# Sample attention: the value blocks' loads are issued by ScalarE instead of SyncE

## The reference, cut to what matters

```python
K = jnp.concatenate([prev_k, k], axis=1)      # 1024 cached + 16 new rows, 8 heads of 64
V = jnp.concatenate([prev_v, v], axis=1)
F = jnp.cumsum(jnp.concatenate([prev_logf, logf], axis=1), axis=1)
s = jnp.einsum('bqhd,bkhd->bhqk', q, K) * scale
s = s + fblk[..., None] - fkT                 # forget terms
s = jnp.where(k_pos <= q_pos, s, -jnp.inf)
p = jax.nn.softmax(s, axis=-1)
o = jnp.einsum('bhqk,bkhd->bqhd', p, V)
b = o * silu(ag)                              # then concatenated, and x + mixed @ w_out
```

## Time and profile before

| | us |
|---|---|
| median of 3 runs | 1608.34 (1605.97 to 1609.19) |
| the profiled execution | 1604.41 |
| its span, first to last instruction | 1602.6 |
| PE busy | 1536.1 (96%) |
| DVE busy | 821.8 (51%) |
| ACT busy | 631.3 (39%) |
| POOL busy | 410.6 (26%) |
| mean granted clock of PE | 0.987 of 2.4 GHz |

### The profile page before, as it was taken

How to read it: one execution, slowest core, us unless ns; L and a number is a source line. 1 busy time by engine, 2 the same in 40 slices (tenths; PEclk the granted TensorE clock), 3 DMA queues, 4 the chain that set the end, 5 groups by cost and what they waited for, 6 DMA issues and landing times.

```text
span 1602.6 us, 24609 instructions
## 1 busy us (share of the span) xinstructions
PE 1536.1 (96%) x9264; PEld 1355.1 (85%) x9264; DVE 821.8 (51%) x2069; ACT 631.3 (39%) x1347; POOL 410.6 (26%) x706
## 2 busy tenths in 40 slices
PE   6999999999999899999999999999998999899999
PEld 5998888878799899898888888888887778688887
DVE  3333112232444422214988988888896788832221
ACT  4443121121211201113877877877975444410100
POOL 1110005555400000022444444444423355200000
PEclk9999999999999899999999999999999999899999
DMA  5433122121110200422133233233233665634441
GB/s 150 149 108 100 42 87 76 47 92 53 62 51 20 70 19 11 85 44 49 36 76 64 58 69 71 49 67 72 49 116 113 222 217 184 238 109 141 129 148 66
DMA packets 181511, 144.63 MB, mean 90 GB/s; under 512 B 104016, under 2 KB 140785, under 8 KB 181393
## 3 DMA queue, kind: packets, MB, share of 16 engines
q1 hardware_dynamic: 178880, 134.08, 28.8%
q10 hardware_dynamic: 2448, 8.91, 1.4%
q0 software_dynamic: 64, 0.07, 0.1%
HBM read 106.50 MB, written 36.53 MB: 89 GB/s over the span
## 4 chain that ended last, share of the span: by engine, by line
PE 52%; DVE 6%; ACT 4%; DMA 2%; issue 2%; POOL 1%; SPq 0%; ACTq 0%; POOLq 0%
PE banks L2263 12%; PE banks L920 12%; PE banks L1546 6%; PE banks L1537 4%; PE banks L1532 3%; PE banks L1562 3%; PE banks L1563 3%; DVE sa_v_lo L1920 2%; PE banks L2021 2%; PE banks L2002 2%; PE banks L1515 2%; ACT pa_s_ring L1386 1%; ACT pa_pt_hi L1415 1%; DMA pa_q_raw<-scratch_q 1%; PE banks L2051 1%
## 5 line engine op out<-in xcount | busy, mean ns | idle before, releaser
L914 PE MATMUL banks<-in_w_hi,in_xt_hi 128*128 128x512 f32 (+1 forms) x680 | 242.4, 356 | 4.6 <-DVE in_w_lo L644 3.1
L914 PE MATMUL banks<-in_w_hi,in_xt_lo 128*128 128x512 f32 (+1 forms) x680 | 239.6, 352 | 0.0
L914 PE MATMUL banks<-in_w_lo,in_xt_hi 128*128 128x512 f32 (+1 forms) x680 | 238.7, 351 | 0.0
L1436 DVE CUSTOM_DVE_ANT_0 pa_s_ring<-banks,pa_f_b 128x512 f32<-128x512 f32 (+2 forms) x320 | 193.2, 604 | 35.8 <-PE banks L1537 33.1
L920 PE MATMUL banks<-in_xt_hi,in_w_hi 128*128 128x384 f32 (+1 forms) x576 | 196.7, 342 | 8.2 <-DVE in_w_lo L644 8.0
L1484 DVE TENSOR_TENSOR pa_pt_lo<-banks,pa_pt_hi 128x512 fp32r<-128x512 f32 (+2 forms) x320 | 193.0, 606 | 21.3 <-ACT pa_pt_hi L1415 18.7
L920 PE MATMUL banks<-in_xt_hi,in_w_lo 128*128 128x384 f32 (+1 forms) x576 | 191.9, 333 | 0.0
L920 PE MATMUL banks<-in_xt_lo,in_w_hi 128*128 128x384 f32 (+1 forms) x576 | 191.8, 333 | 0.0
L1415 ACT ACTIVATE pa_pt_hi<-banks 128x512 fp32r<-128x512 f32 (+2 forms) x320 | 166.6, 534 | 54.1 <-PE banks L1546 52.9
L1546 PE MATMUL banks<-ident,pa_s_ring 128*128 128x128 f32 x1088 | 174.0, 275 | 9.7 <-DVE pa_pt_lo L1484 4.2
L1562 PE MATMUL banks<-pa_pt_hi,pa_vs 128*128 128x256 f32 x576 | 163.6, 300 | 0.4 <-DVE pa_parts L1464 0.3
(11 more groups left out here) (245 smaller groups left out, 2810.8 us busy)
## 6 DMA issues: line engine op xcount, KB each, us to landing
sa_k_c<-in_cache_k_dram SPq DMA_DIRECT2D x8, 2048.0 KB, 9.8
sa_v_c<-in_cache_v_dram SPq DMA_DIRECT2D x8, 2048.0 KB, 8.2
in_w_raw<-in_w_in_dram SPq DMA_DIRECT2D x48, 256.0 KB, 3.7
out_dram<-in_out SPq DMA_DIRECT2D x34, 256.0 KB, 2.0
out_dram<-op_y ACTq DMA_DIRECT2D x17, 512.0 KB, 5.1
in_x<-in_x_prompt_dram SPq DMA_DIRECT2D x16, 512.0 KB, 3.5
op_x<-in_x_prompt_dram SPq DMA_DIRECT2D x16, 512.0 KB, 4.9
pa_f_b<-scratch_f SPq DMA_DIRECT2D x28, 256.0 KB, 5.2
```

The costliest lines, as they stand in the source:

```text
L914: mm = pe.matmul(ps[:, u % NBANK, 0:n], tile_of(xa, t)[:, k, :], wa[:, k, c0:c0 + n], start=(k == 0 and q == 0), stop=(k == KT - 1 and q = ...
L1436: done = dve.tensor_tensor_reduce(scores_of(j)[:, b * P:(b + nb) * P], ps_s[:, (h * NQD + at) % 3, 0:nb * P], f_b[h % 2][:, b * P:(b + nb) ...
```

## The change

The value loads of blocks 1 to 7 leave SP's stream and go into ACT's, behind `high_k` of chunk 2 and in front of `high_p` of the block before. The two waits that protect the single buffer `v_c`, on `vn_done` and `vl_done`, go with them. The load of block 0 stays in SP's stream, as do the keys, the forget sums, the weights and the stores. Amounts, buffers and everything on PE, DVE and POOL stay the same.

```diff
+    def load_v(eng, b):
+        eng.dma_start(v_c[:, :, :],
+                      cache_v[b * PAST:(b + 1) * PAST, :].rearrange("(t p) d -> p t d", p=P)).then_inc(v_in, 16)
+        eng.dma_start(v_n[0:NQ, :], new_v[b * NQ:(b + 1) * NQ, :]).then_inc(v_in, 16)
+
     def on_sp(sp, step, weights):
...
         if step == "rings_dead":
-            load_v(0)
+            load_v(sp, 0)
             return
...
                 sp.wait_ge(k_turned, (b + 1) * KB)
                 load_k(b + 2, par)
-            if b + 1 < NB:
-
-                sp.wait_ge(vn_done, b + 1)
-                sp.wait_ge(vl_done, 4 * (b + 1))
-                load_v(b + 1)
             if b + 2 < NB:
 
                 sp.wait_ge(scored, (b + 1) * NC_)
...
         for b in range(NB):
             high_k(b, 2)
             if b:
+                act.wait_ge(vn_done, b)
+                act.wait_ge(vl_done, 4 * b)
+                load_v(act, b)
                 high_p(b - 1, (0, 1))
```

More of the change, by code:

```diff
@@ L1728, in load_f @@
                              f_t_all[b * H + part * NB * H:(b + 1) * H + part * NB * H, 0:PAST + NQ]).then_inc(f_in[par], 16)
[L1730 to L1733, removed]
         def store(b, par):
```

## The result

| | before | after |
|---|---|---|
| median of 5 runs, us | 1606.8 (1605.6 to 1609.2) | 1676.3 (1674.0 to 1679.5) |
| span of the profiled execution, us | 1602.6 | 1674.7 |
| PE busy | 96% | 93% |
| mean granted clock of PE | 0.987 | 0.964 |

The ratio is 1.043, 95% interval 1.0415 to 1.0445: the change costs 69.5 us between medians. The span of the profiled executions grew by 72.1 us; the forecast was 74.4 us and 1682 us.

What follows compares the result with a forecast made beforehand. The value loop, with about 1 us to spare, was taken to bound the block once the load is late: 8.0 + 183.6 - 117.2 = 74.4 us on 1608.3, about 1682 us; own range 1666 to 1694, stated range 1644 to 1704.

Steps and rivals of the forecast that it cites:

- What bounds: Sample attention: loop of value buffer, load, POOL and DVE nearly as long as the block; load hidden with about 1 us spare.
- Place: Value load issued behind ACT's chunk 2 copies, 5.2 us later a block; this lateness alone costs 38.7 us.
- Company: Value loads share the DMA engines with keys or weights: issue to POOL's start 14.4 us in place of 9.3.
- Both ways to the number: Two estimates of value load issue to POOL's start under sharing: 14.7 us and 14.3 us; 14.4 taken.
- the pair of block 1: Value and key loads issued close together in the kernel before: 14.8 us for both, less 0.5 us is 14.3.
- Weights in blocks 6 and 7: Output weights go out beside the values there, 2 MB each, so these loads are charged the same 14.4 us.
- Clock: PE idles about 10 us a block, its clock falls to half; transposes and scores on the loop cost 1.1 us a block.
- Rival 3: PE at half clock for the whole block becomes the bound: 34 us a block, +94.8 us, 1703 us; chance 12%.
- Sum: Block 1 is 8.0 us late, blocks 1 to 7 take 183.6 us against 117.2: 74.4 us more.
- lower bound of my range: 13.2 us to POOL and no clock loss: 28.1 us a block, +58 us, 1666 us.
- Median: Median of runs taken 3.9 us above the profiled execution, 1608.3 us; plus 74.4 gives about 1682 us.
- Costed at nothing: ACT's two issues, about 1 us, covered by PE's idle time; also SP's earlier forget sums and output store.

Runs made afterwards that it cites:

- early ACT kernel: Against the changed kernel, ACT issues the value load of block b+1 right behind the exponentials of block b, ahead of its chunk 2 copies; 1605.7 us.
- kernel with the keys held back: As the changed kernel, but SP waits for the block's value load to land before issuing the keys or the weights; 1634.2 us.
- half load: As the changed kernel, but from block 1 on only the first half of each cached value block is loaded, 1 MB in place of 2; 1645.4 us.
- pairs in one queue: Against the changed kernel, SP issues the value loads at the keys' late time: behind the keys 1673.8 us, ahead of them 1636.8 us.
- fills: Changed kernel plus 60 unused PE transposes from block 2 on, before the wait for chunk 2's third bank: 1677.0 us; also with new value rows issued first: 1674.6 us.

## Why the prediction was right, point by point

- **What bounds.** Right: the value loop had about 1 us to spare, and SP's 100 us of waiting cost nothing. The early ACT kernel shows that the engine which issues is indifferent. The kernel with the keys held back shows that the delay of the place goes into the block: the issue comes 6.1 us later behind the start of `low_v` (11.6 against 5.5), 1.0 us of that was covered, the load is 0.6 us shorter, and the block is 4.4 us longer (23.9 against 19.5).
- **Place.** The issue moved where the working said, behind the fourth copy. It even leaves 0.06 us after this copy starts (1282.38 against 1282.32) and not after it ends: ACT issues the transfer while the copy runs. That is 0.4 us a block less than I charged. With the keys out of the way the place costs 28 us between medians; I had 38.7 (25.5 us a block; measured 23.9). The miss per block is the issue (0.4 us), the load (8.7 us against 9.3), and about 0.5 us less of clock loss.
- **Company.** 14.4 us taken, 14.5 measured, in seven loads of 13.6 to 15.6 us. Both ways to the number, the 5.9 us that the second 2 MB took behind the first and the pair of block 1, were good. Both took it that the two queues share the same DMA engines, and that is what the half load and the pairs in one queue bear out. The keys and the values were issued 0.07 us apart and not 0.5. With 0.07 my formula gives 9.3 + 5.9 - 0.07 = 15.1 us, so that 14.5 was met so closely is in part luck: the issue was 0.4 us off one way, the sharing about 0.6 us the other.
- **Weights in blocks 6 and 7.** Charged as the keys, 14.4 us; measured 13.6 and 14.1 us.
- **Clock.** 1.1 us a block charged on the loop. From the start of `low_v` to the end of the fourth copy it is 12.35 us, against the 11.3 us that I had without the clock: 1.05 us, of which 0.8 lie between the third and the fourth copy (1.90 us apart and not 1.11). The fills give back 1.1 us where the clock is still up at the fourth copy. Rival 3 (half clock throughout) fell: in every block from 2 on the clock came back 4.5 to 7.3 us after PE resumed. One row was misread: in the stretch of the earlier trace rows the clock does not come back after 6 us of work, it is at half throughout; in the trace it is back from 1255 on, 8.5 us after PE resumed at 1246.4. It served only as an argument against rival 3, and the sum does not rest on it.
- **Sum.** `low_v(1)` starts 6.4 us later than before. I had 8.0: in this execution the fourth copy of block 1 came at 1252.1 and not at 1253.4, in a stage whose first value load was issued 2.8 us earlier, and the load left 0.4 us sooner after the copy. Blocks 1 to 7, from one `low_v` to the other (1270.37 to 1451.62 us): 181.3 us against 117.2, +64.1 (I had 66.4). Behind `low_v(7)`: 223.1 us against 221.4, +1.7, for which I had nothing. 6.4 + 64.1 + 1.7 = 72.2, the 72.1 us of the span up to rounding. The lower bound of my range has a slip: with 13.2 us to POOL the block is 28.3 us and not 28.1, which moves 1666 to 1668 us.
- **Median.** Of the 5.7 us by which 1682 is too high, 2.4 us are the sum's (1678.8 us forecast for the execution, 1676.4 measured). The rest, rounding aside, is that I added 3.9 us from one execution to the median; the changed kernel's profiled execution is its median, and with five executions the median of before is 1606.8 and not 1608.3.
- **Costed at nothing.** ACT's 1 us of issuing: nothing, as the early ACT kernel shows even without the late load's cover.

## What to carry to other kernels

A transfer's place in the stream of the engine that issues it decides when it leaves: before moving a load to another engine, find the instruction ahead of it there, what that one waits for, and how much cover the load had. Then look at what else is issued at that moment; here two loads of 2 MB within 0.1 us of each other took 12 to 14 us each in place of 8 to 9, and with both in one queue it was the second that bore it. A long wait on an engine that only issues transfers is no loss in itself.

## What the runs showed of the hardware

- Two queues are served side by side: 12.1 and 13.4 us for 2 MB each, against 7.9 to 8.6 us alone. In one queue it is 8.2 us for the first and 13.0 us for the second.
- The fourth of four transfers on one queue, 32 KB behind 4 MB, took 3.4 to 3.7 us to issue, and the second of the four mostly 0.6. With the pair spread over two queues the last issue took 0.7 us or less in five blocks of seven, 1.4 at most. This is what a second issuer saves. Here it won nothing: with one queue, values behind keys, the time was 1673.8 us against 1676.3.
- A transfer of 32 KB issued ahead of the 2 MB lands in 3.6 us beside the keys, behind them in 13.8.
- ACT issues a transfer while its own copy runs: 0.06 us after the start of a copy of 0.40 us.
